# Padded rows for x, interleaved feed-forward rows, and the three split products in a new order

## The reference

```python
def half_ffn(x, g, w_in, w_out):
    gate, up = split(rms_norm(x, g) @ w_in, 2)
    return x + 0.5 * (silu(gate) * up) @ w_out

for i in range(2):                      # DEPTH
    y = half_ffn(y, ffn_norm1[i], ffn_w_in1[i], ffn_w_out1[i])
    h = rms_norm(y, mix_norm[i])
    y = y + (mlstm_mixer(h) if i == 0 else windowed_attention(h))
    y = half_ffn(y, ffn_norm2[i], ffn_w_in2[i], ffn_w_out2[i])
return rms_norm(y, final_norm), new states, new keys and values
```

## Time and profile before

| | us |
|---|---|
| median of 3 runs | 1104.1 |
| lowest, highest | 1103.12, 1105.3 |
| profiled execution, its own time | 1104.89 |
| span of the profile | 1103.0 |
| TensorE busy in the span | 1086.1 (98%) |
| VectorE busy | 692.7 (63%) |
| ScalarE busy | 520.9 (47%) |

### The profile page before, as it was taken

One profiled execution on the slowest core, in us unless ns is written; L12 is line 12 of the kernel. 1 busy time (PEld: TensorE's weight loads), 2 busy tenths in 40 slices (PEclk: granted clock), 3 DMA queues, 4 the chain that ended last, 5 costly groups with the idle time before them and its releaser, 6 DMA issues.

```text
span 1103.0 us, 21261 instructions
## 1 busy us (share of the span) xinstructions
PE 1086.1 (98%) x8086; PEld 1068.1 (97%) x8086; DVE 692.7 (63%) x1071; ACT 520.9 (47%) x812; POOL 124.7 (11%) x158
## 2 busy tenths in 40 slices
PE   8999999999999999999999999999999999999997
PEld 7999999998999999999999999999988899999997
DVE  6766665465656766665547666645599776666441
ACT  6544443345665544443335444433466554444332
POOL 5000001100004300000110000011232500000011
PEclk9999999999999999999999999999999999999999
DMA  6544454324333644554434444544332244444531
GB/s 229 193 178 162 152 210 158 133 110 181 130 125 125 203 172 159 179 185 160 164 143 153 166 176 152 202 156 151 132 124 90 109 160 158 180 156 181 179 136 43
DMA packets 24435, 172.43 MB, mean 156 GB/s; under 512 B 3236, under 2 KB 3400, under 8 KB 5832
## 3 DMA queue, kind: packets, MB, share of 16 engines
q1 hardware_dynamic: 22368, 167.45, 42.7%
q0 software_dynamic: 1248, 2.92, 0.7%
q10 hardware_dynamic: 776, 1.48, 0.4%
HBM read 169.28 MB, written 2.57 MB: 156 GB/s over the span
## 4 chain that ended last, share of the span: by engine, by line
PE 92%; DVE 4%; DMA 2%; ACT 2%; issue 1%; SPq 0%; POOL 0%; DVEq 0%; ACTq 0%
PE acc L402 30%; PE acc L404 29%; PE acc L403 29%; DMA raw<-in_w 2%; DVE wlo L389 1%; PE mb L662 0%; ACT whi L365 0%; PE mb L681 0%; DVE rstd L1036 0%; PE mb L588 0%; PE acc L709 0%; ACT work L949 0%; PE mb L423 0%; PE num L597 0%; DVE work L1258 0%
## 5 line engine op out<-in xcount | busy, mean ns | idle before, releaser
L402 PE MATMUL acc<-xhi,whi 128*128 128x288 f32 x1696 | 507.0, 299 | 3.9 <-DVE wlo L389 2.0
L403 PE MATMUL acc<-xlo,whi 128*128 128x288 f32 x1696 | 501.1, 295 | 0.0
L365 ACT ACTIVATE whi<-raw 128x1024 fp32r<-128x1024 f32 (+1 forms) x290 | 326.7, 1128 | 366.5 <-PE acc L404 338.2
L404 PE MATMUL acc<-xhi,wlo 128*128 128x288 f32 x1696 | 499.5, 295 | 0.0
L389 DVE TENSOR_TENSOR wlo<-raw,whi 128x1024 fp32r<-128x1024 f32 (+1 forms) x290 | 386.2, 1332 | 167.9 <-ACT whi L365 157.1
L402 PEld LDWEIGHTS acc<-xhi,whi 128*128 128x128 f32 x1696 | 318.5, 188 | 6.6 <-DVE wlo L389 2.2
L404 PEld LDWEIGHTS acc<-xhi,wlo 128*128 128x128 f32 x1696 | 320.2, 189 | 0.0
L403 PEld LDWEIGHTS acc<-xlo,whi 128*128 128x128 f32 x1696 | 319.3, 188 | 0.5
L402 PE MATMUL acc<-ahi,whi 128*128 128x288 f32 x832 | 247.2, 297 | 0.9 <-DVE alo L1270 0.7
L403 PE MATMUL acc<-alo,whi 128*128 128x288 f32 x832 | 245.4, 295 | 0.0
L404 PE MATMUL acc<-ahi,wlo 128*128 128x288 f32 x832 | 244.6, 294 | 0.0
(11 more groups left out here) (227 smaller groups left out, 606.9 us busy)
## 6 DMA issues: line engine op xcount, KB each, us to landing
raw<-in_w SPq DMA_DIRECT2D x113, 1024.0 KB, 4.8
raw<-in_w SPq DMA_DIRECT2D x32, 1408.0 KB, 5.9
x<-in_xT SPq DMA_DIRECT2D x4, 288.0 KB, 6.8
raw<-in_w SPq DMA_DIRECT2D x4, 256.0 KB, 6.0
work<-row_bounce ACTq DMA_DIRECT2D x1, 640.0 KB, 4.3
work<-in_cst POOLq DMA_DIRECT2D x1, 560.0 KB, 4.2
work<-in_c POOLq DMA_DIRECT2D x1, 514.0 KB, 4.3
out_cp<-work POOLq DMA_DIRECT2D x4, 128.5 KB, 3.9
```

The source lines that it names most:

```text
L365: act.activation(dst, src, ACT.Copy).then_inc(hi_done, 1)
L402: pe.matmul(out, wh, hi[:, k, :], start=(first and n == 0), stop=False)
L403: pe.matmul(out, wh, lo[:, k, :], start=False, stop=False)
L404: mm = pe.matmul(out, wl, hi[:, k, :], start=False, stop=(last and n == len(tiles) - 1))
```

## The change

Three edits, all on the moving operand of the products.

1. xhi and xlo become the two halves of one tile, `xs`, whose rows are 320 tokens long (1,280 bytes), of which the first 288 are used.
2. ahi and alo become one tile, `fs`, in which row k of alo lies directly behind row k of ahi.
3. `products` takes a tuple of passes. Each pass goes over all tiles of the call and issues the products it names. Six stages get a new tuple. The row's wait is issued when a row is first met.

```diff
+TX = 320
+PASSES = {0: ("hh hl lh",), 1: ("hh hl lh",), 2: ("hh hl lh",), 4: ("lh hh hl",), 5: ("lh hh hl",), 6: ("hh hl", "lh"), 7: ("hh hl", "lh"), 8: ("hh hl lh",), 10: ("hh", "hl", "lh"), 11: ("hh", "hl", "lh")}
...
-        xhi = sb("xhi", [P, KD, T], F32R)
-        xlo = sb("xlo", [P, KD, T], F32R)
-        ahi = sb("ahi", [P, KF, T], F32R)
-        alo = sb("alo", [P, KF, T], F32R)
+        xs = sb("xs", [P, 2, KD, TX], F32R)
+        xhi, xlo = xs[:, 0, :, 0:T], xs[:, 1, :, 0:T]
+        fs = sb("fs", [P, KF, 2, T], F32R)
+        ahi, alo = fs[:, :, 0, :], fs[:, :, 1, :]
...
-        def products(pe, out, slot, tiles, hi, lo, first, last, before=None):
-
-            for n, (t, k) in enumerate(tiles):
-                if before:
-                    before(k)
-                wh, wl = whi[:, slot, t, :], wlo[:, slot, t, :]
-                pe.matmul(out, wh, hi[:, k, :], start=(first and n == 0), stop=False)
-                pe.matmul(out, wh, lo[:, k, :], start=False, stop=False)
-                mm = pe.matmul(out, wl, hi[:, k, :], start=False, stop=(last and n == len(tiles) - 1))
+        def products(pe, out, slot, tiles, hi, lo, first, last, before=None, passes=("hh hl lh",)):
+
+            total, n, seen = 3 * len(tiles), 0, set()
+            for names in passes:
+                for t, k in tiles:
+                    if before and k not in seen:
+                        before(k)
+                    seen.add(k)
+                    for name in names.split():
+                        wt = (whi if name[0] == "h" else wlo)[:, slot, t, :]
+                        xt = (hi if name[1] == "h" else lo)[:, k, :]
+                        mm = pe.matmul(out, wt, xt, start=(first and n == 0), stop=(last and n == total - 1))
+                        n += 1
             return mm
```

More of the change, by code:

```diff
@@ L450, in in_piece @@
                     pe.wait_ge(evac, 4 * it + G - 3)
-                products(pe, group_bank(g), c % 4, [(k, k) for k in range(KD)], xhi, xlo, True, True).then_inc(piece_done, 1)
+                products(pe, group_bank(g), c % 4, [(k, k) for k in range(KD)], xhi, xlo, True, True, None, PASSES[i]).then_inc(piece_done, 1)
             def first_two(i, c, G):
@@ L461, in first_two @@
                         mm = products(pe, group_bank(q), (c + q) % 4, [(k, k) for k in ks], xhi, xlo,
-                                      ks[0] == 0, ks[-1] == KD - 1, before=x_ready if q == 0 else None)
+                                      ks[0] == 0, ks[-1] == KD - 1, x_ready if q == 0 else None, PASSES[i])
                         if ks[-1] == KD - 1:
@@ L506, in unit @@
                         products(pe, acc[u][:, 0:T], c % 4, [(t, t + 11 * q) for t in range(11)], ahi, alo,
-                                 q == 0, q == 1, before).then_inc(piece_done, 1)
+                                 q == 0, q == 1, before, PASSES[i]).then_inc(piece_done, 1)
                 unit(0, 0, before=lambda k: pe.wait_ge(alo_done, n_alo[0] + k + 1))
```

## The result

The changed kernel takes 1094.4 us (median of 4 runs, 1093.5 to 1096.3) against 1104.7 of before on the same chip: a ratio of 0.9911, 95% interval 0.9898 to 0.9923. The forecast was no change, 1098 to 1108. It was wrong: the kernel is 10 us faster, on the side to which I had given 0.17.

What follows compares the result with a forecast made beforehand. TensorE's stream of 7,584 products 133.3 ns apart was taken as the bound. The profiled 1104.89 us + 0 + 0 + 0 (order, writers, reads), or 1104.1 us taken from the median, was forecast, range 1098 to 1108.

Steps and rivals of the forecast that it cites:

- The bound: Whole kernel: TensorE busy 98% of the span, 7,584 products 133.3 ns apart, six stages without a wait.
- The order at 0: Stages 4, 5, 6, 7, 10 and 11: reordering adds no instruction and rows are ready in time; cost 0.
- no wait for alo at the heads of stages 7 and 11: Stages 7 and 11: row 21's alo comes 3.67 us in, wanted at 7.07 and 5.73 us; a wait in stage 11 had chance 0.03.
- The slack of row 7 in stage 10: Stage 10's head: row 7 still asked for after 42 products, at 886.89, its xlo ending at 885.35.
- The writers at 0: Writers of x and feed-forward rows: cost unchanged; for L926 and L1270, bounds 0 and + 0.6 us, 0 taken.
- The read side at 0: TensorE's moving reads: new row places leave 133.3 ns unchanged; bounds 101 us less and + 25 us, 0 taken.
- The signs that I had named: Stages 5 or 7 differing by over 0.2 us means distance; changes in stages keeping their order mean layout alone.
- only positions that were there before: Moving reads: x rows at multiples of 256, feed-forward rows at multiples of 128, all already among the old starts.
- The rival that came true: Moving reads and weight loads stop colliding: 101, 68 or 28 us less by which products gain; chance 0.17.
- A partial effect of 1 ns: Within the faster rival: 1 ns less on all products, 7.6 us, giving 1096.5.
- Its counter-argument: Against the faster rival: the 13.3 ns are equal for every start seen.
- The slower rival's price: Moving reads meet a new conflict: up to 5 ns on 5,088 products, 1129, or on 1696, 1112.6; chance 0.10.

Runs made afterwards that it cites:

- Kernel 1: Changed kernel with the old order of the products in every stage, so the layout alone; 1094.5 us, ratio 0.990 against before.
- runs 1 and 9: Run 1 is Kernel 1; run 9 is the changed layout in the old order with spacer tiles ahead of and behind xs: 1104.6 us, ratio 1.0001.
- run 2: Changed kernel with the four old tiles, so the new order alone; 1103.7 us, ratio 0.9986 against before.
- Blocks 0/0, 128/0 and the one in groups of three: Unused products added behind Kernel 1's last stage, by moving/weight start; the third alternates starts 0 and 128 in threes: 131.67, 133.33, 133.33 ns a product.
- the block at 148: 72 unused products behind the last stage of the changed layout in the old order, moving start 148: 140.0 ns a product.
- kernel 11: Changed layout in the old order, x rows starting at 144 and fs at 16 and 144 modulo 256; 1086.3 us, ratio 0.9829 against before.
- kernel 10: Changed layout in the old order, x rows starting at 144 modulo 256, fs unmoved; 1088.0 us, ratio 0.9851 against before.
- kernels 10 to 12: Shifts inside the tile; kernel 10 and kernel 11 have own lines, the last has padded x rows at 128 modulo 256, old order: 1102.5 us, ratio 0.9975.

## Why the prediction was wrong

**The bound** was read rightly: TensorE's stream of 7,584 products at one distance, with no waits in six stages. So was the scale: a change of 0.29 ns a product would be measurable. The distance fell by 1.67 ns on 5,088 products with x (8.5 us), and by 1.0 to 1.2 on the 2,112 of the feed-forward output (2.2 us). Together 10.7; the spans differ by 9.1, since stage 4 has a new wait, stage 2 a stretch at the lower clock, and stage 8, full of other work, gained nothing (60.5 us from its first product to its last both times).

**The order at 0** was right for this layout. Kernel 1 and the changed kernel have the same time, and there is no wait for alo at the heads of stages 7 and 11. The slack of row 7 in stage 10 held as well. What I missed was stage 4, where row 7 had only 0.28 us of slack; the wait there costs 0.9 us, and runs 1 and 9 show that neither the order nor the faster products are needed for it. On the old layout the order alone took 1.0 us off (run 2).

**The writers at 0** was right: L1276, the stepped write of four rows, takes 286 ns against 288.

**The read side at 0 is the step that failed.** Its premise held: the old rows take every multiple of 128 modulo 2,048. So did its observation, that all starts are equally far apart. The inference did not: I took equal distances for proof that no place is better than another. Blocks 0/0, 128/0 and the one in groups of three show why. A product's pace is not its own: where rows at 0 and at 128 follow each other in equal groups of up to three, all of them have the slower distance, and no single start in the trace of before shows the faster one. My sample contained every place and not one run of equal places. The signs that I had named did point to the distance: stages 5 and 7 are 0.55 and 0.62 us shorter, and stage 1, whose order is unchanged, went from 70.39 to 69.85. The sentence "only positions that were there before" was true and worth nothing.

**The rival that came true**, a read conflict that goes, was rightly made and priced too coarsely. Its price was the whole surplus of 13.3 ns, which nothing here removes: 12.5% of it went (1.67 of 13.3), 25% at the best place found. "A partial effect of 1 ns" was nearest. Its counter-argument carried the same faulty inference, and with it the chance of 0.17.

**The slower rival's price**, up to 5 ns for a product from L584, was no upper bound either: the block at 148 costs 140.0, 6.7 ns more than 133.33. No row of the change lies so.

**What stays open.** That the place of the moving row against the weight tile counts is shown, and that their relative place modulo 256 sets the distance for starts on multiples of 128, as long as all starts are alike. That the two reads collide is only the likeliest reading, and how they would is not shown. The surplus does not scale with the width of the weight tile, four bytes can matter more than a hundred, and one place can have two steady distances: kernel 11's stage 0 takes 143.20 us where kernel 10's takes 141.88, with the x rows in the same place (120.03 and 118.76 of it from 30 us on, 131.1 and 130.0 ns for a product). No run here tells which mechanism that is, and no block tried had less than 130.0 ns for 288 columns.

## What to carry to other kernels

Equal spacing in a trace tells how a pattern runs, not that its parts are indifferent: to learn whether a place matters, make a run in which only that place occurs. Where TensorE is the bound, a few blocks of products behind the kernel's last stage measure dozens of layouts in one run. The stages of kernels 10 to 12 then followed them to a tenth of a nanosecond; stage 11 of kernel 2 did not, as no block had its pattern. Moving rows at well-chosen places relative to the weight tiles are worth 1.5 to 1.7% here, for some 2.5 KB in each partition; check the address that the tile really gets.

## What the runs showed of the hardware

- The distance between fp32r products with 128 weight columns exceeds one column a cycle by 10.0 to 13.3 ns in the six widths shown, from 256 to 512 columns (120.0 ns for both 256 and 264).
- At 288 columns it depends on where the moving row and the weight tile start: 131.67 ns with both at 0 or both at 128 modulo 256, 133.33 with one of them moved by 128, 130.0 to 131.1 at 144 against 0, 140.0 at 148 against 0.
- Alternating between a good and a bad start, singly or in threes, has the distance of the bad one for all (133.33 ns); in twelves, or with one bad start in three, it has the mean (132.5 and 132.2 ns).
- The granted clock can fall to its lower level in one kernel's profile and not in another's at the same work: 0.51 from 246.40 to 249.80 us in the changed kernel, 1.00 there before. TensorE had waited 2.16 us for `wlo` (L391) just ahead of it, and 2.00 us (L389) before. In kernel 11 it was 0.51 from 847.70 to 851.10 us, in stage 9, after waits of 0.51 and 0.73 us (PEclk 0.95 over the 36.50 us from 831.53); in kernel 10 it was 1.00 throughout that stage (35.10 us), with waits of the same length.
